# Decoder step: where a gate bias is added, where one weight split and one group of sums of squares stand

## The chip, the cores and the metric

The kernel runs on one core of one Trainium2 chip. The metric is the device time of one execution in microseconds (us), the median of several runs. TensorE (PE) does the matrix products, VectorE (DVE) and ScalarE (ACT) work element by element, GpSimd (POOL) and SyncE (SP) here mostly start transfers (DMA). Each engine runs its own list of instructions in order; semaphores make one wait for another. SBUF is the memory on the core, PSUM the memory into which TensorE writes.

## The reference, cut to what matters

Two layers over 256 prompt rows and 64 sample rows (8 sequences of 8), width 1024, all float32. The change touches the first half of a layer:

```python
z = h @ w_in[l]
u = gelu(z[..., :512]); v_raw = gelu(z[..., 512:1024]); p = z[..., 1024:]
# chunk_sgu: 4 heads x 128
v = head_layernorm(v_raw, g, b)
mixed = einsum('hts,bnshd->bnthd', w, vc) + bias      # bias = sgu_b[h, t]
ya = u * mixed
yb = pool_mix(...)                                    # windows 2/4/8/16, then a 128x128 product per group
mix = concatenate([rmsnorm(ya, branch_a_g), rmsnorm(yb, branch_b_g)]) @ w_out[l]
x = x + gt1 * mix
```

After it come a second norm and a SwiGLU, dense in layer 0, top-2-of-8 experts in layer 1.

## The kernel before

Activations lie transposed, channels on partitions and the 320 tokens along the free dimension. Every large weight matrix is read in units of 512x512 (1 MB) into a ring of six buffers `raw` by SP. ScalarE rounds a unit to `w_hi` (lines 709, 715), VectorE subtracts to get the remainder `w_lo` (lines 1052, 1057), and TensorE makes three products for each part: `w_hi` by the high part of the activation, `w_hi` by its low part, `w_lo` by the high part. `hi_to(s)` and `lo_to(s)` in the code mean: split all units up to number s that are not yet split, and where such a call stands in an engine's list decides what waits behind it. Units of `ada_w` are used as they are ("plain", line 1669, `ada`).

A layer's mixer half goes like this.

`project_in` multiplies six units, c = 0, 1, 2 for the pooling branch, v and u, two each, called j = 0 to 5. Ahead of unit j = 3 TensorE makes three of the four small products of the pooling branch (`mix_pool`, lines 1828 and 1829), which need VectorE's window differences (`pooled`, lines 1232 to 1246, semaphore `d_done`). `pooled` itself waits for ScalarE's copies of p (`p_out`, lines 810 to 815) and, half way, for GpSimd's window sums of the samples (`win_s`, line 621). On VectorE `lo_to(s + 4)`, the split of unit j = 3, stands ahead of `pooled`.

`mixer` makes the four heads of the gate (`mix_gate`). For a head: a product of a row of ones with the bias row for the 256 prompt columns (line 1814), the two products with the masked `gw` (1817), the bias product for the 64 sample columns (1819) and the sample product (1821). The bias row `g_bias` lies on one partition of `pst`. In layer 1 `mod_rows` (lines 1835, 1837) stands between heads 0 and 1; in layer 0 two `ada` units stand behind head 0 and two behind head 1. Behind the last head TensorE counts up `gate_mm`, on which VectorE forms `ya = u * gate` in one instruction (line 1278, reading PSUM), counts up `ya_done`, and goes on; ScalarE squares `ya` (line 861).

`project_out` multiplies four units of `w_out`, q = 0 to 3. The first two (q = 0, 1) take the rows of yb, which are ready; the last two take the rows of ya, which need its norm. Inside q = 0, after two of its four 128-row steps k (12 products each), TensorE waits for `ya_done` and the squares and makes their sums (`sum_squares`, line 1686), and in layer 0 the transposes of `ada_tr` (line 1679). Then ScalarE takes the root (741), VectorE the reciprocal (1252) and the scaled ya (1254), ScalarE and VectorE split it (795, 1264), and unit q = 2 can start.

GpSimd loads each layer's small parameters with `load_layer`; that of layer 1 starts when `gate_mm` says that layer 0's are used.

Of the kernel before, what the change touches and what calls it, by code (L numbers as in the profile page):

```python
# [30 lines left out]
P = 128  # L31
# [4 lines left out]
NSEQ = 8  # L36
# [13 lines left out]
BIAS_ROW = 96  # L50
# [96 lines left out]
def write_program(nc, ctx, d, o):  # L147
# [64 lines left out]
    g_bias = pst[BIAS_ROW:BIAS_ROW + 1].rearrange("p (h t) -> p h t", t=P)  # L212
# [345 lines left out]
    def _(gp):  # L558
# [8 lines left out]
        def load_layer(l):  # L567

            gp.dma_start(pw[:], d['pool_w'][l].rearrange("g c e -> c g e")).then_inc(layer_in, 16)
            gp.dma_start(g_bias, d['sgu_b'][l:l + 1]).then_inc(layer_in, 16)  # L570
            gp.dma_start(vng[:], d['v_norm_g'][l].partition_broadcast(P)).then_inc(layer_in, 16)
            gp.dma_start(vnb[:], d['v_norm_b'][l].partition_broadcast(P)).then_inc(layer_in, 16)
# [42 lines left out]
        for l in range(DEPTH):  # L615
# [18 lines left out]
            if l + 1 < DEPTH:  # L634
                gp.wait_ge(gate_mm, l + 1)
# [402 lines left out]
    def _(ve):  # L1038
# [146 lines left out]
        def project_in(l):  # L1185
# [10 lines left out]
            lo_to(s + 4)  # L1196
# [70 lines left out]
        def mixer(l):  # L1267
# [7 lines left out]
            branch_lo(H, 4 * l)  # L1275
            lo_to(S_OUT[l] + 3)
            ve.wait_ge(gate_mm, l + 1)
            v.tensor_tensor(uT[:], uT[:], ps[:, 0:H, 0:T], ALU.mult).then_inc(ya_done, 1)
# [363 lines left out]
    def _(pe):  # L1642
# [168 lines left out]
        def mix_gate(l, h):  # L1811
            hc = slice(h * P, (h + 1) * P)
            bias_one = ones[BIAS_ROW:BIAS_ROW + 1, :]
            t_.matmul(ps[:, h, 0:NP_TOK], bias_one, g_bias[:, h, :].unsqueeze(1).to_broadcast([1, 2, P]), start=True,
                      stop=False)
            for n in range(2):
                t_.matmul(ps[:, h, n * P:(n + 1) * P], v_norm[:, n, hc], gw[:, l, h, :], start=False, stop=(n == 1))
            tk = slice(NP_TOK, T)
            t_.matmul(ps[:, h, tk], bias_one, g_bias[:, h, 0:TS].unsqueeze(1).to_broadcast([1, NSEQ, TS]),
                      start=True, stop=False)  # L1820
            ins = t_.matmul(ps[:, h, tk], v_norm[NS_TOK:P, 2, hc], gs[NS_TOK:P, l, h, :], start=False, stop=True)
            if h == H - 1:
                ins.then_inc(gate_mm, 1)
# [32 lines left out]
        def project_out(l):  # L1856
# [7 lines left out]
            for q, (r, c) in enumerate(OUT_ORDER):  # L1864
# [13 lines left out]
                if q < N_OUT - 1:  # L1878
                    for k in range(KB):
                        if q == 0 and k == 2:  # L1880
                            pe.wait_ge(ya_done, l + 1)
                            sum_squares(12 * l + 2, 0, H, 0)
                            if l == 0:
                                ada_tr(SELF_B[0])
                        for m in range(4):
# [245 lines left out]
```

## Time and profile before

| | us |
|---|---|
| median of 3 runs | 1590.06 |
| lowest, highest | 1585.67, 1593.28 |
| profiled execution, its own time | 1592.71 |
| its span in the trace | 1591.0 |
| TensorE busy in the span | 1541.1 (97%) |
| VectorE, ScalarE busy | 1183.0, 946.6 |
| mean granted TensorE clock | 0.977 |

Layer 0's mixer half takes the first 160 us, the dense SwiGLU goes to about 470 us, layer 1's mixer half from there to about 595 us, and the experts take the rest. The trace gives start and duration of each instruction; matmuls overlap, so the distance between starts tells more than the duration. A float32 product (the gate, the sums of squares) shows as two matmul records, so "x4" there is two products. The granted clock is 1.00 at 2.4 GHz and 0.50 at 1.2 GHz. Times are counted from the start of the span.

### The profile page before, as it was taken

To read this page: it belongs to the slowest core of one execution; us is meant where nothing else is said; L and a number is where in the kernel's file an instruction comes from. 1 tells how busy PE (TensorE), PEld (TensorE's weight loads), DVE (VectorE), ACT (ScalarE), POOL (GpSimd) and SP (SyncE) were. 2 spreads that over 40 slices of the span, in tenths; PEclk is the share of its full clock that TensorE was granted. 3 is DMA by queue.
4 is the path that set the end of the run, shared out by engine and by line. 5 is a ranking of instruction groups with operands and counts; after the bars stand their busy time and mean duration, and the time that the engine had idled before them with its cause. 6 is when DMAs were issued, how large, how long until landed. Compare 5 with 4: busy or idle time off the path is not lost.

```text
span 1591.0 us, 21820 instructions
## 1 busy us (share of the span) xinstructions
PE 1541.1 (97%) x8061; PEld 1306.7 (82%) x8061; DVE 1183.0 (74%) x969; ACT 946.6 (59%) x721; POOL 70.7 (4%) x115
## 2 busy tenths in 40 slices
PE   6899999999998997999999999999999999999997
PEld 3669799999986796888888888888888888888785
DVE  3465544444465656888898898888888888889897
ACT  3343432333324534777777777777777777777774
POOL 4100000000000001000000000000000000001001
PEclk8999999999999996999999999999999999999999
DMA  9966764444439474999999999999999999999993
GB/s 344 377 241 251 293 244 136 154 158 133 157 110 382 149 255 133 377 375 370 390 381 370 394 379 366 400 372 377 392 371 371 403 371 373 395 374 367 398 377 134
DMA packets 234538, 493.00 MB, mean 310 GB/s; under 512 B 10219, under 2 KB 16235, under 8 KB 229370
## 3 DMA queue, kind: packets, MB, share of 16 engines
q1 hardware_dynamic: 226086, 472.82, 80.9%
q0 software_dynamic: 6112, 19.10, 3.2%
q10 hardware_dynamic: 2308, 0.64, 0.2%
q8 instruction: 21, 0.34, 0.1%
q14 instruction: 11, 0.09, 0.0%
HBM read 482.39 MB, written 10.36 MB: 310 GB/s over the span
## 4 chain that ended last, share of the span: by engine, by line
PE 90%; DMA 4%; DVE 3%; ACT 1%; issue 1%; SPq 0%; ACTq 0%; DVEq 0%
PE ps L1647 19%; PE ps L1649 19%; PE ps L1648 19%; PE ps L1915 4%; PE ps L1916 4%; PE ps L1917 4%; PE ps L1925 2%; PE ps L1926 2%; PE ps L1927 2%; DMA raw<-in_w_in 2%; PE ps L2068 2%; DMA raw<-in_ada_w 1%; PE ps L1874 1%; PE ps L1669 1%; PE ps L1875 1%; PE ps L1876 1%
## 5 line engine op out<-in xcount | busy, mean ns | idle before, releaser
L1057 DVE TENSOR_TENSOR w_lo<-raw,w_hi 128x2048 fp32r<-128x2048 f32 x366 | 835.2, 2291 | 178.9 <-ACT w_hi L715 177.7
L715 ACT ACTIVATE w_hi<-raw 128x2048 fp32r<-128x2048 f32 x366 | 701.9, 1918 | 263.7 <-PE ps L1649 162.1
L1647 PE MATMUL ps<-w_hi,split 128*128 128x512 f32 x1392 | 550.8, 396 | 2.1 <-DVE sp_ L1096 1.5
L1649 PE MATMUL ps<-w_hi,split 128*128 128x512 f32 x1392 | 544.0, 391 | 0.0
L1648 PE MATMUL ps<-w_lo,split 128*128 128x512 f32 x1392 | 543.6, 391 | 0.0
L1647 PEld LDWEIGHTS ps<-w_hi,split 128*128 128x128 f32 x1392 | 262.7, 189 | 58.8 <-DVE w_lo L1057 4.1
L1649 PEld LDWEIGHTS ps<-w_hi,split 128*128 128x128 f32 x1392 | 262.4, 189 | 55.6
L1648 PEld LDWEIGHTS ps<-w_lo,split 128*128 128x128 f32 x1392 | 262.9, 189 | 52.4
L1915 PE MATMUL ps<-split,w_hi 128*128 128x320 f32 x448 | 138.7, 310 | 1.9 <-DVE split L1162 1.9
L1917 PE MATMUL ps<-split,w_lo 128*128 128x320 f32 x448 | 138.4, 309 | 0.0
L1916 PE MATMUL ps<-split,w_hi 128*128 128x320 f32 x448 | 138.4, 309 | 0.0
L1052 DVE TENSOR_TENSOR w_lo<-raw,w_hi 128x2048 fp32r<-128x2048 f32 x32 | 73.3, 2293 | 69.9 <-ACT w_hi L709 69.9
L709 ACT ACTIVATE w_hi<-raw 128x2048 fp32r<-128x2048 f32 x32 | 60.9, 1908 | 51.2 <-PE ps L1917 17.1
L1915 PEld LDWEIGHTS ps<-split,w_hi 128*128 128x128 f32 x448 | 84.1, 188 | 3.6 <-issue 3.6
L1916 PEld LDWEIGHTS ps<-split,w_hi 128*128 128x128 f32 x448 | 84.1, 188 | 0.0
L1917 PEld LDWEIGHTS ps<-split,w_lo 128*128 128x128 f32 x448 | 84.1, 188 | 0.0
L983 ACT ACTIVATE split<-ps 128x512 fp32r<-128x512 f32 x56 | 33.5, 598 | 63.4 <-PE ps L2068 63.4
L1925 PE MATMUL ps<-split,w_hi 128*128 128x320 f32 x208 | 64.3, 309 | 0.0
L1926 PE MATMUL ps<-split,w_hi 128*128 128x320 f32 x208 | 64.3, 309 | 0.0
L1927 PE MATMUL ps<-split,w_lo 128*128 128x320 f32 x208 | 64.3, 309 | 0.0
L1669 PE MATMUL ps<-raw,cT 128*32 128x512 f32 x384 | 48.3, 623 | 8.8 <-DMA raw<-in_ada_w 8.8
L1800 PE MATMUL ps<-split,w_hi 128*128 128x320 f32 x128 | 41.7, 326 | 3.4 <-DVE split L1162 1.8
(342 smaller groups left out, 1297.8 us busy)
## 6 DMA issues: line engine op xcount, KB each, us to landing
raw<-in_moe_w SPq DMA_DIRECT2D x336, 1024.0 KB, 7.3
raw<-in_ffn_w SPq DMA_DIRECT2D x42, 1024.0 KB, 5.0
raw<-in_ada_w SPq DMA_DIRECT2D x40, 1024.0 KB, 7.2
raw<-in_w_in SPq DMA_DIRECT2D x12, 1024.0 KB, 11.0
raw<-in_ada_w SPq DMA_DIRECT2D x16, 512.0 KB, 10.7
raw<-in_w_out SPq DMA_DIRECT2D x8, 1024.0 KB, 8.9
item_rows<-plain POOLq DMA_DIRECT2D x12, 512.0 KB, 7.8
plain<-in_x_prompt SPq DMA_DIRECT2D x2, 512.0 KB, 3.8
```

The costliest lines, as they stand in the source:

```text
L715: a.activation(w_hi[:, (s0 + j) % SPL], raw[:, (u0 + j) % RAW], ACT.Copy).then_inc(hi_ready, 1)
L1052: v.tensor_tensor(w_lo[:, s % SPL], raw[:, u % RAW], w_hi[:, s % SPL].bitcast(F32), ALU.subtract).then_inc(lo_ready, 1)
L1057: v.tensor_tensor(w_lo[:, (s0 + j) % SPL], raw[:, (u0 + j) % RAW], w_hi[:, (s0 + j) % SPL].bitcast(F32), ALU.subtract).then_inc(lo_ready, 1)
L1647: t_.matmul(out, a_hi, b_hi, start=first_, stop=False)
L1648: t_.matmul(out, a_hi, b_lo, start=False, stop=False)
L1649: return t_.matmul(out, a_lo, b_hi, start=False, stop=last_)
L1915: t_.matmul(out, wh[:, k, mc], h_hi[:, kk, 0:T], start=(kk == 0), stop=False)
L1916: t_.matmul(out, wh[:, k, mc], h_lo[:, kk, 0:T], start=False, stop=False)
L1917: ins = t_.matmul(out, wl[:, k, mc], h_hi[:, kk, 0:T], start=False, stop=(kk == KD - 1))
L1925: t_.matmul(out, wh[:, k, mc], gh[:, k, :], start=(k == 0), stop=False)
L1926: t_.matmul(out, wh[:, k, mc], gl[:, k, :], start=False, stop=False)
L1927: ins = t_.matmul(out, wl[:, k, mc], gh[:, k, :], start=False, stop=(k == KB - 1))
```

## The change

The bias goes to a buffer of its own that holds it on all 128 partitions, loaded by a transfer that repeats the row. The two bias products of each head are gone. VectorE adds the bias to the gate in two instructions (256 prompt columns and 64 sample columns of each of four heads), waits for them, and then multiplies with u. This block stands ahead of the split of output unit q = 2 (`lo_to(S_OUT[l] + 3)`) and behind that of q = 1; before, the product stood behind both. GpSimd's `load_layer(1)` waits for `ya_done`, since VectorE now reads the bias. On TensorE the sums of squares stand after three steps k of unit q = 0, with `ada_tr` ahead of them. And in `project_in` the call `lo_to(s + 4)` ahead of `pooled` is made in layer 0 alone; in layer 1 the split of unit j = 3 falls behind `pooled`.

```diff
-    g_bias = pst[BIAS_ROW:BIAS_ROW + 1].rearrange("p (h t) -> p h t", t=P)
+    g_bias = sb("g_bias", [P, H, P])
...
-            gp.dma_start(g_bias, d['sgu_b'][l:l + 1]).then_inc(layer_in, 16)
+            gp.dma_start(g_bias[:].rearrange("p h t -> p (h t)"),
+                         d['sgu_b'][l].rearrange("h t -> (h t)").partition_broadcast(P)).then_inc(layer_in, 16)
...
-                gp.wait_ge(gate_mm, l + 1)
+                gp.wait_ge(ya_done, l + 1)
...
-            lo_to(s + 4)
+            if l == 0:
+                lo_to(s + 4)
             pooled(l)
...
             branch_lo(H, 4 * l)
+            lo_to(S_OUT[l] + 2)
+            ve.wait_ge(gate_mm, l + 1)
+            gated = hf[:, 0:H, :]
+            v.tensor_tensor(gated[:, :, 0:NP_TOK].rearrange("p h (n t) -> p h n t", t=P),
+                            ps[:, 0:H, 0:NP_TOK].rearrange("p h (n t) -> p h n t", t=P),
+                            g_bias[:].unsqueeze(2).to_broadcast([P, H, 2, P]), ALU.add)
+            step(v.tensor_tensor(gated[:, :, NP_TOK:T].rearrange("p h (n t) -> p h n t", t=TS),
+                                 ps[:, 0:H, NP_TOK:T].rearrange("p h (n t) -> p h n t", t=TS),
+                                 g_bias[:, :, 0:TS].unsqueeze(2).to_broadcast([P, H, NSEQ, TS]), ALU.add))
+            v.tensor_tensor(uT[:], uT[:], gated, ALU.mult).then_inc(ya_done, 1)
             lo_to(S_OUT[l] + 3)
-            ve.wait_ge(gate_mm, l + 1)
-            v.tensor_tensor(uT[:], uT[:], ps[:, 0:H, 0:T], ALU.mult).then_inc(ya_done, 1)
...
-            t_.matmul(ps[:, h, 0:NP_TOK], bias_one, g_bias[:, h, :].unsqueeze(1).to_broadcast([1, 2, P]), start=True,
-                      stop=False)
             for n in range(2):
-                t_.matmul(ps[:, h, n * P:(n + 1) * P], v_norm[:, n, hc], gw[:, l, h, :], start=False, stop=(n == 1))
-            tk = slice(NP_TOK, T)
-            t_.matmul(ps[:, h, tk], bias_one, g_bias[:, h, 0:TS].unsqueeze(1).to_broadcast([1, NSEQ, TS]),
-                      start=True, stop=False)
-            ins = t_.matmul(ps[:, h, tk], v_norm[NS_TOK:P, 2, hc], gs[NS_TOK:P, l, h, :], start=False, stop=True)
+                t_.matmul(ps[:, h, n * P:(n + 1) * P], v_norm[:, n, hc], gw[:, l, h, :], start=True, stop=True)
+            ins = t_.matmul(ps[:, h, NP_TOK:T], v_norm[NS_TOK:P, 2, hc], gs[NS_TOK:P, l, h, :], start=True, stop=True)
...
-                        if q == 0 and k == 2:
+                        if q == 0 and k == 3:
                             pe.wait_ge(ya_done, l + 1)
-                            sum_squares(12 * l + 2, 0, H, 0)
                             if l == 0:
                                 ada_tr(SELF_B[0])
+                            sum_squares(12 * l + 2, 0, H, 0)
```

On VectorE in layer 1, around the pooling differences. Before, with the splits of j = 2 and j = 3 as "x2":

```order
L1052 TENSOR_TENSOR w_lo<-raw,w_hi 128x2048 x2
L1232 TENSOR_TENSOR plain<-pp 128x4x270
L1232 TENSOR_TENSOR plain<-plain 128x3x268
L1232 TENSOR_TENSOR plain<-plain 128x2x264
L1232 TENSOR_TENSOR plain<-plain 128x256
L1238 SCALAR_TENSOR_TENSOR plain<-plain,pp 128x240
```

After, where `pooled` ends and the splits of j = 3 and j = 4 follow as "x2" (its start has one split ahead of it):

```order
L1239 SCALAR_TENSOR_TENSOR plain<-plain,pp 128x240
L1241 SCALAR_TENSOR_TENSOR plain<-plain,sp_ 128x8x8
L1243 TENSOR_TENSOR first<-plain,rcnt 128x16
L1247 TENSOR_TENSOR plain<-first,pp 128x16 x4
L1052 TENSOR_TENSOR w_lo<-raw,w_hi 128x2048 x2
L1204 BN_STATS v_stat<-plain 128x6 x12
```

One split has moved from ahead of `pooled` to behind it.

On TensorE in layer 1, from the last transposes of `project_in` to gate head 1. `ps<-pst,ones` is a bias product, `ps<-mix,plain` a gate product. Before:

```order
L1814 MATMUL ps<-pst,ones 128x256
L1817 MATMUL ps<-mix,plain 128x128 x2
L1819 MATMUL ps<-pst,ones 128x64
L1821 MATMUL ps<-mix,plain 128x64
L1835 MATMUL ps<-ident,gain 72x128
L1835 MATMUL ps<-ident,mod 72x128 x2
L1837 MATMUL ps<-rw,mod 9x8 x8
L1814 MATMUL ps<-pst,ones 128x256
```

After:

```order
L1823 MATMUL ps<-mix,plain 128x128 x2
L1824 MATMUL ps<-mix,plain 128x64
L1838 MATMUL ps<-ident,gain 72x128
L1838 MATMUL ps<-ident,mod 72x128 x2
L1840 MATMUL ps<-rw,mod 9x8 x8
L1823 MATMUL ps<-mix,plain 128x128 x2
```

Both bias products are gone from each head.

On TensorE in layer 0, inside output unit q = 0 (`w_hi` and `w_lo` with `split` are its products). Before, where the unit's first product is row 331:

```order
353 L1875 MATMUL ps<-split,w_hi 128x320
354 L1876 MATMUL ps<-split,w_lo 128x320
355 L1686 MATMUL ps<-hf,ones 128x320 x4
356 L1679 MATMUL ps<-ident,modrow 128x128 x4
357 L1874 MATMUL ps<-split,w_hi 128x320
```

After, where its first product is row 323:

```order
357 L1878 MATMUL ps<-split,w_hi 128x320
358 L1879 MATMUL ps<-split,w_lo 128x320
359 L1688 MATMUL ps<-ident,modrow 128x128 x4
360 L1695 MATMUL ps<-hf,ones 128x320 x4
361 L1877 MATMUL ps<-split,w_hi 128x320
```

The sums have moved from behind 24 products to behind 36, and the transposes stand ahead of them.

## Rows read from the trace of the kernel before

**Rows 1.** Page, part 1: engine, busy us, share of the span, instructions.

```profile
PE 1541.1 (97%) x8061; PEld 1306.7 (82%) x8061; DVE 1183.0 (74%) x969; ACT 946.6 (59%) x721; POOL 70.7 (4%) x115
```

**Rows 2.** Groups by line, 600 to 1591 us: busy, mean ns, idle before by releaser.

```profile
L715 ACT ACTIVATE w_hi<-raw 128x2048 fp32r<-128x2048 f32 x334 | 640.7, 1918 | 166.0 <-PE ps L1649 162.1 <-DMA raw<-in_moe_w 3.7 <-issue 0.3
L1647 PE MATMUL ps<-w_hi,split 128*128 128x512 f32 x1344 | 530.6, 395 | 0.6 <-DVE w_lo L1057 0.6
```

**Rows 3.** Timelines of ACT, POOL, DVE and PE around layer 1's `pooled`: start, us.

```profile
499.15 0.28 ACT L815 ACTIVATE hf<-ps 128x60 f32<-128x60 f32 x1
500.95 2.12 POOL L621 TENSOR_TENSOR plain<-plain 128x480 f32<-128x480 f32 x3
503.86 2.29 DVE L1052 TENSOR_TENSOR w_lo<-raw,w_hi 128x2048 fp32r<-128x2048 f32 x1 [5.93 <-ACT w_hi L709]
506.07 1.28 DVE L1232 TENSOR_TENSOR plain<-pp 128x1080 f32<-128x1080 f32 x1
511.90 0.43 DVE L1246 TENSOR_TENSOR plain<-first,pp 128x16 f32<-128x16 f32 x4
512.38 0.70 PE L1828 MATMUL ps<-plain,mix 128*128 128x256 f32 x2 [2.76 <-DVE plain L1246]
```

**Rows 4.** Stretches: length, busy of PE, PEld, DVE, ACT, POOL, granted clock, DMA, GB/s.

```profile
20.00:40.00 20.00, 11.79 (x67) 6.62 (x68) 8.78 (x14) 5.95 (x8) 4.23 (x7) 0.74 1.06 378
...
124.00:132.00 8.00, 8.00 (x33) 7.56 (x33) 3.69 (x2) 3.08 (x4) 2.43 (x4) 0.57 1.04 412
...
513.00:518.00 5.00, 5.00 (x20) 4.21 (x19) 0.26 (x1) 3.65 (x5) 0.00 (x0) 0.66 1.01 406
547.00:551.00 4.00, 3.02 (x31) 2.13 (x30) 3.79 (x6) 2.19 (x3) 0.00 (x0) 1.00 0.00 0
551.00:565.00 14.00, 14.00 (x46) 10.67 (x45) 6.62 (x4) 6.06 (x7) 0.00 (x0) 0.51 0.69 156
```

**Rows 5.** Timeline of PE in layer 0, gate heads 2 and 3.

```profile
120.00 1.06 PE L1669 MATMUL ps<-raw,cT 128*32 128x512 f32 x8 [1.36 <-DMA raw<-in_ada_w]
120.99 0.69 PE L1814 MATMUL ps<-pst,ones 1*128 1x256 f32 x2
121.62 0.71 PE L1817 MATMUL ps<-mix,plain 128*128 128x128 f32 x4
122.26 0.43 PE L1819 MATMUL ps<-pst,ones 1*128 1x64 f32 x2
122.62 0.43 PE L1821 MATMUL ps<-mix,plain 64*128 64x64 f32 x2
```

**Rows 6.** Timeline of PE in layer 1: gate, output unit q = 0, sums.

```profile
548.08 0.67 PE L1814 MATMUL ps<-pst,ones 1*128 1x256 f32 x2 [0.98 <-ACT plain L848]
...
561.43 0.63 PE L1874 MATMUL ps<-split,w_hi 128*128 128x320 f32 x1
...
566.57 2.31 PE L1686 MATMUL ps<-hf,ones 128*128 128x320 f32 x8
...
569.16 0.30 PE L1874 MATMUL ps<-split,w_hi 128*128 128x320 f32 x1
...
577.08 0.31 PE L1874 MATMUL ps<-split,w_hi 128*128 128x320 f32 x1
```

**Rows 7.** Timelines of DVE and ACT in layer 1, from the gate's end.

```profile
553.45 4.50 DVE L1052 TENSOR_TENSOR w_lo<-raw,w_hi 128x2048 fp32r<-128x2048 f32 x2 [1.81 <-ACT w_hi L709]
561.53 1.49 DVE L1278 TENSOR_TENSOR plain<-plain,ps 128x1280 f32<-128x1280 f32 x1 [3.59 <-PE ps L1821]
569.48 2.15 DVE L1252 RECIPROCAL rstd<-rstd 128x320 f32<-128x320 f32 x1 [6.46 <-ACT rstd L741]
573.53 1.72 DVE L1264 TENSOR_TENSOR split<-hf,split 128x640 fp32r<-128x640 f32 x2
563.05 1.36 ACT L861 ACTIVATE hf<-plain 128x640 f32<-128x640 f32 x2 [7.84 <-DVE plain L1278]
```

**Rows 8.** Chain of work that ended last, in order of time: start, us, what.

```profile
49.31 13.53 DMA raw<-in_w_in
```

More of the change, by code:

```diff
@@ L49 @@
 WIN = (2, 4, 8, 16)
-BIAS_ROW = 96
 PADP = 16
@@ L1812, in mix_gate @@
             hc = slice(h * P, (h + 1) * P)
-            bias_one = ones[BIAS_ROW:BIAS_ROW + 1, :]
-            t_.matmul(ps[:, h, 0:NP_TOK], bias_one, g_bias[:, h, :].unsqueeze(1).to_broadcast([1, 2, P]), start=True,
-                      stop=False)
             for n in range(2):
-                t_.matmul(ps[:, h, n * P:(n + 1) * P], v_norm[:, n, hc], gw[:, l, h, :], start=False, stop=(n == 1))
-            tk = slice(NP_TOK, T)
-            t_.matmul(ps[:, h, tk], bias_one, g_bias[:, h, 0:TS].unsqueeze(1).to_broadcast([1, NSEQ, TS]),
-                      start=True, stop=False)
-            ins = t_.matmul(ps[:, h, tk], v_norm[NS_TOK:P, 2, hc], gs[NS_TOK:P, l, h, :], start=False, stop=True)
+                t_.matmul(ps[:, h, n * P:(n + 1) * P], v_norm[:, n, hc], gw[:, l, h, :], start=True, stop=True)
+            ins = t_.matmul(ps[:, h, NP_TOK:T], v_norm[NS_TOK:P, 2, hc], gs[NS_TOK:P, l, h, :], start=True, stop=True)
             if h == H - 1:
```

## The prediction, made before the changed kernel was run

> **What bounds the kernel now.** I read the engines' busy times first, then who waits for whom, then the timeline of each stretch that the diff touches. TensorE is busy 97% of the span [rows 1]. In the experts it idles 0.6 us over 1344 products of a line, and ScalarE waits for it (162 us), not for weights (3.7 us) [rows 2]. So whatever TensorE gains ahead of the experts reaches the end, unless something takes it back on the way. Two of its losses matter here. It idles 2.76 us in layer 1 for VectorE's pooling differences [rows 3]. And its clock falls from 2.4 to 1.2 GHz (granted share 0.5) in three stretches beside the change [rows 4]: 124 to 132 us at a mean of 0.57, that is 2 x 0.43 x 8 = 6.9 us at the low level; 513 to 518 at 0.66, 3.4 us; 551 to 565 at 0.51, 13.7 us. Time at the low level costs at most half of itself.
>
> **The pooling differences in layer 1.** Before, the split of unit j = 3 waits 5.93 us for ScalarE and runs 503.86 to 506.15, and `pooled` runs 506.07 to 512.33 [rows 3]. What `pooled` itself needs is there earlier: ScalarE's copies at 499.43, GpSimd's sums at 503.07 [rows 3]. Without the split ahead of it, it ends by 503.1 + 6.3 = 509.4 even if all of it waited for the sums, and near 506 if its first half runs before them. TensorE comes free 2.76 us before 512.38, at 509.6, so this idle time goes: **2.8 us**. What is late next is the split of j = 3: it ends 2.3 us behind `pooled`, at 508.3 (at 511.7 at worst). TensorE needs it behind three pooling products, 512.38 to 515.11 at part low clock, near 2.1 us at full, so at 511.7. No wait. SP's next load hangs on TensorE's `ada` units there, at 508.8, not on this split. The low clock from 513 on followed that idle time with TensorE otherwise at work; with it gone I count its 3.4 us x 0.5 = **1.6 us** as saved too. Together 4.4; between 2.8 and 4.5.
>
> **The bias products.** A head's first costs 121.62 - 120.99 = 0.63 us and its second 122.62 - 122.26 = 0.36 us at full clock [rows 5], together 0.99. Layer 1 has four heads with nothing between them but `mod_rows`: 3.96 us. In layer 0 heads 0 and 1 lie ahead of an `ada` unit whose load lands at 120.0, where TensorE already waits 1.36 us [rows 5]; the transfers are saturated there, and their issue lies ahead of the gate. Their 1.98 us only lengthen that wait. Heads 2 and 3 lie behind it: **2.0 us**.
>
> **The clock in layer 1.** From 547 to 551 TensorE idles 0.98 us and is else busy with small gate products, and it is at the low level from 551 to 565: through three heads and half of unit q = 0, until the large products have run for 3 us [rows 4, 6]. After the change the thin stretch shrinks from 548.1-561.4 to 548.1-553.0 at full clock (4.0 for four bare heads, 0.9 for `mod_rows`). The nearest row of such a length is layer 0's, with 6.9 us at the low level; I take that. Saved: (13.7 - 6.9) x 0.5 = 3.4. The bounds are 0 (it stays low as long) and 6.8 (it does not fall). With 3.96 that makes **7.4 us** for layer 1's gate. In layer 0 I leave the clock as it was, though its thin stretch changes too: TensorE waits 3.3 us in all for loads in place of 1.4, and then has less thin work; bounds 3.4 either way.
>
> The Trainium skill (TensorE: Matmul & The Clock Gate, section "Why this matters for your kernels") says that the clock drops after an idle gap between bursts of matmuls. The idle gap of 2.76 us bears that out; the fall at 551, after 0.98 us of idle and with products in every other slot, does not. By that rule alone, layer 1's gate would stay at full clock.
>
> **VectorE's added steps.** The old product takes 1.49 us for 1280 columns read from PSUM, and 640 columns take 0.86 (two in 1.72) [rows 7]. By these the adds of 1024 and 256 columns take near 1.2 and 0.4, 1.6 together with a wait, and the product 1.5: **3.1 us** from `gate_mm` to `ya_done`, off TensorE's path if covered. In layer 1: the second of the splits at 553.45 now stands behind, the first moves up with `mod_rows` by 1.0, to end near 554.8; `ya_done` near 557.9, squares (1.36, [rows 7]) near 559.3. TensorE starts q = 0 at 553.0 and makes 36 products. At full clock 54 products take 577.08 - 569.16 = 7.92 us [rows 6], 0.147 each, so 36 take 5.3: arrival 558.3, plus 3.4 for low clock = 561.7. Cover 2.4 us; at full clock a wait of 1.0. In layer 0 the split of q = 2 no longer stands ahead, adds and squares take 4.5, and 36 products take 5.3 or more: covered. That split comes up to 3 us later, for a unit that TensorE reaches over 10 us later. Waiting here also are GpSimd's loads for layer 1, needed 350 us on, and ScalarE's squares.
>
> **The sums one step later.** They cost TensorE the same. What gets shorter is the cover of the root, reciprocal, scaling and split behind them: 575.25 - 568.9 = 6.3 us [rows 7]. TensorE has 12 + 48 products left ahead of q = 2, 8.8 us. Before it had 72, 10.6. Cost 0, cover 2.5. If VectorE were 2.5 us late there it would be the path.
>
> **The larger load.** 256 KB in place of 2 KB, in layer 0 at 32 us, when the transfers run at 378 GB/s and a share of 1.06 [rows 4]. The chain goes through such a load later, 49.31 to 62.84 [rows 8]. 0.254 MB by 378 GB/s is **0.7 us**, lost; bounds 0 and 1.4 (if the repeated row goes at half the rate). Layer 1's copy is in nobody's way.
>
> **Sum.** 4.4 + 2.0 + 7.4 - 0.7 = 13.1 us off. The profiled execution took 1592.7, 2.65 above the median of 1590.06; by its own time it would be 1579.6. Against the median: **1577.0 us**.
>
> **Rivals.** (a) The clock does not fall in layer 1's gate, since the small products keep it up. The saving is 6.8 in place of 3.4 and the wait for the squares costs 1.0: 1574.6; if layer 0's does not fall either, 3.4 less, 1571.2. For it: the stretch is a third as long. Against it: the fall at 551 came 3 us into such work. The Trainium skill (TensorE: Matmul & The Clock Gate, "Why this matters for your kernels"), which names idle gaps alone, would give (a) for layer 1. (b) The clock gives nothing back: low in layer 1 up to the same products (3.4 more), and in layer 0 also during the loads' wait (3.4 more): 1577.0 + 6.8 = 1583.8. For it: layer 0 now idles 3.3 us where 2.76 went with a fall [rows 3, 4]. Against it: the large products come 8 us sooner in layer 1. (c) The idle time before the pooling products only changes its releaser, to the split of j = 3 or the row sums: 4.4 back, 1581.4. Against it are the times above. (d) The gain is lost in the experts, where the transfers are nearly full: 1590. Against it stands the 0.6 us [rows 2]. (e) Slower: the add with a repeated operand runs at the rate of VectorE's slowest row, the reciprocal, 2.15 us for 320 columns [rows 7]. The adds then take 8.6 in place of 1.6. In layer 1 the squares end 7.0 later, 4.6 behind TensorE's arrival at 561.7. In layer 0 the gate's end to the squares takes 11.5 against 8.7 of products with the low clock: 2.8. Two waits of that size each bring back up to 3.4 of low clock: 4.6 + 2.8 + 6.8 = 14.2, more than the 13.1 saved: 1591.2. It decides from about 8 us for the adds on. Against it: the same kind of instruction with PSUM takes 1.49 for 1280.
>
> **How the numbers follow.** The forecast 0.52, (a) 0.13, (b) 0.18, (c) 0.06, (d) 0.06, (e) 0.05. About 8 us, 0.5%, is what a measurement of this kernel can tell from no change, so faster means under 1582.1: the forecast, (a), (c) and half of (b) hold 0.80, from which I take 0.03 for scatter of the median: 0.77. Within 0.5%: the rest of (b), (d), most of (e): 0.20. Slower 0.03. The range goes from (a)'s lower end, 1571, to 1585, past (b); (d), (e) and scatter, under 0.2, are left out.
>
> **What would show it.** In the profile of after: no idle time ahead of layer 1's first pooling product and a clock of 1.00 behind it, or (c). Between the starts of two neighbouring heads 1.0 us. Adds of 1.2 and 0.4 us, or (e). No idle time ahead of either layer's sums of squares and of unit q = 2; a wait there means that VectorE's chain is the path. The low clock near layer 1's gate 3 to 7 us long; 13 is (b), none is (a). TensorE's wait in layer 0's second pair of `ada` units near 3.3 us. The first large products some 0.7 us later up to 80 us. What would prove me wrong altogether: the experts lasting longer than before by what was gained.

## The result and the profile after

| | us |
|---|---|
| before, same chip, 4 runs | 1590.60 (1585.67 to 1593.28) |
| after, 4 runs | 1573.58 (1571.84 to 1577.49) |
| ratio | 0.9914, 95% interval 0.9895 to 0.9934 |
| profiled execution of after, its span | 1577.49, 1575.7 |

The change takes 17.0 us off the median, where 13.1 were forecast. The profiled pair lies 15.2 us apart, which is what the traces have to explain.

First the page of after, part 1, which answers to [rows 1], and the groups by line from 600 us on, which answer to [rows 2].

```profile
PE 1528.3 (97%) x8029; PEld 1297.2 (82%) x8029; DVE 1188.1 (75%) x973; ACT 946.5 (60%) x721; POOL 73.4 (5%) x115
...
L715 ACT ACTIVATE w_hi<-raw 128x2048 fp32r<-128x2048 f32 x334 | 640.7, 1918 | 165.4 <-PE ps L1658 163.0 <-DMA raw<-in_moe_w 2.0 <-issue 0.3
```

TensorE has 32 records and 12.8 us less to do, VectorE 4 instructions and 5.1 us more. In the experts ScalarE still waits 163 us for TensorE and 2.0 us for weights. So TensorE is the bound there as before.

**Where the time went.** I cut the span at eight starts that both kernels have on TensorE. These rows are of before (start, duration, engine, line, what): the `ada` unit ahead of layer 0's pooling products, the one ahead of its gate, the sums of x behind unit q = 3, the `ada` units ahead of and behind layer 1's unit j = 3, and the transposes of x behind layer 1's mixer. Between the first two stands the start of layer 0's pooling products. Layer 1's gate begins at 548.08 [rows 6].

```profile
69.20 1.92 PE L1669 MATMUL ps<-raw,cT 128*32 128x512 f32 x16
73.91 1.22 PE L1828 MATMUL ps<-plain,mix 128*128 128x256 f32 x2 [2.78 <-DVE plain L1246]
109.89 1.92 PE L1669 MATMUL ps<-raw,cT 128*32 128x512 f32 x16
158.84 0.43 PE L1686 MATMUL ps<-hf,ones 128*128 128x320 f32 x1
507.70 1.50 PE L1669 MATMUL ps<-raw,cT 128*32 128x512 f32 x12
524.36 1.06 PE L1669 MATMUL ps<-raw,cT 128*32 128x512 f32 x8
593.36 0.49 PE L1987 MATMUL ps<-ident,x 128*128 128x128 f32 x3
```

The same places on TensorE in after, with its gates between them. What stands in brackets is idle time before the row and what ended it.

```profile
71.64 1.92 PE L1678 MATMUL ps<-raw,cT 128*32 128x512 f32 x16
74.75 0.70 PE L1831 MATMUL ps<-plain,mix 128*128 128x256 f32 x2 [1.18 <-DVE plain L1247]
107.78 1.92 PE L1678 MATMUL ps<-raw,cT 128*32 128x512 f32 x16
115.77 1.51 PE L1678 MATMUL ps<-raw,cT 128*32 128x512 f32 x8 [2.20 <-DMA raw<-in_ada_w]
118.25 1.93 PE L1678 MATMUL ps<-raw,cT 128*32 128x512 f32 x8 [0.97 <-DMA raw<-in_ada_w]
155.78 0.43 PE L1695 MATMUL ps<-hf,ones 128*128 128x320 f32 x1
504.64 1.92 PE L1678 MATMUL ps<-raw,cT 128*32 128x512 f32 x16
506.49 0.48 PE L1831 MATMUL ps<-plain,mix 128*128 128x256 f32 x1
516.86 0.64 PE L1678 MATMUL ps<-raw,cT 128*32 128x512 f32 x4
540.58 0.68 PE L1823 MATMUL ps<-mix,plain 128*128 128x128 f32 x4 [0.98 <-ACT plain L848]
578.87 0.38 PE L1990 MATMUL ps<-ident,x 128*128 128x128 f32 x2
```

And in a second trace of after, the same program without an edit, profiled on another chip (1570.36 us by its own time, span 1568.5):

```profile
70.78 1.92 PE L1678 MATMUL ps<-raw,cT 128*32 128x512 f32 x16
108.49 1.92 PE L1678 MATMUL ps<-raw,cT 128*32 128x512 f32 x16
114.97 1.06 PE L1678 MATMUL ps<-raw,cT 128*32 128x512 f32 x8 [0.69 <-DMA raw<-in_ada_w]
117.45 1.07 PE L1678 MATMUL ps<-raw,cT 128*32 128x512 f32 x8 [1.42 <-DMA raw<-in_ada_w]
151.31 0.43 PE L1695 MATMUL ps<-hf,ones 128*128 128x320 f32 x1
501.31 1.92 PE L1678 MATMUL ps<-raw,cT 128*32 128x512 f32 x16
513.53 1.05 PE L1678 MATMUL ps<-raw,cT 128*32 128x512 f32 x6
537.25 0.68 PE L1823 MATMUL ps<-mix,plain 128*128 128x128 f32 x4 [0.98 <-ACT plain L848]
547.84 2.39 PE L1695 MATMUL ps<-hf,ones 128*128 128x320 f32 x8
572.94 0.49 PE L1990 MATMUL ps<-ident,x 128*128 128x128 f32 x3
```

The differences of neighbouring starts, in us:

| stretch | before | after | after, second trace |
|---|---|---|---|
| A: start to layer 0's unit j = 3 | 69.20 | 71.64 | 70.78 |
| B: to layer 0's gate | 40.69 | 36.14 | 37.71 |
| C: layer 0's gate and output product | 48.95 | 48.00 | 42.82 |
| D: to layer 1's unit j = 3 | 348.86 | 348.86 | 350.00 |
| E: pooling products and unit j = 3 | 16.66 | 12.22 | 12.22 |
| F: to layer 1's gate | 23.72 | 23.72 | 23.72 |
| G: layer 1's gate and output product | 45.28 | 38.29 | 35.69 |
| H: to the end | 997.64 | 996.83 | 995.56 |

In the first trace 4.44 us went in E, 6.99 in G, 0.95 in C, 2.11 in A and B together and 0.81 in H. That is the 15.3 us between the spans. F stays the same to 0.01 us, and so does D where the clock is the same.

The last two columns are one program, and they differ by 7.2 us. Most of that is granted clock. These rows are stretches of after, then of its second trace: length, busy time of PE, PEld, DVE, ACT and POOL, granted clock, DMA share, GB/s.

```profile
60.00:66.00 6.00, 4.35 (x12) 3.52 (x13) 1.98 (x4) 1.92 (x1) 4.10 (x5) 0.72 1.03 425
110.00:130.00 20.00, 16.83 (x90) 11.24 (x89) 8.88 (x7) 7.44 (x7) 2.42 (x4) 0.74 1.01 393
540.00:555.00 15.00, 14.42 (x84) 12.69 (x85) 11.65 (x10) 8.47 (x10) 0.00 (x0) 0.77 0.54 131
```

```profile
110.00:130.00 20.00, 17.89 (x119) 12.90 (x116) 10.39 (x10) 8.69 (x9) 2.43 (x4) 1.00 1.01 389
...
470.00:480.00 10.00, 8.12 (x51) 7.24 (x42) 7.09 (x14) 8.95 (x13) 0.00 (x0) 0.83 1.02 411
```

A mean of 0.74 over 20 us is 2 x 0.26 x 20 = 10.4 us at 1.2 GHz. The first trace has 3.4, 10.4 and 6.9 us at this level in the three stretches. The second has none there and 3.4 us at 470. What the low level costs can be read where TensorE makes the same work with and without it:

| same work | with low clock | without | cost |
|---|---|---|---|
| G, both traces of after | 38.29, 6.9 low | 35.69 | 2.60 |
| C from the last `ada` load (118.25, 117.45) on, both traces of after | 37.53, 8.2 low | 33.86 | 3.67 |
| layer 0's pooling products to the gate's `ada` unit, before and first after | 35.98, 6.8 low | 33.03 | 2.95 |

That is 0.38 to 0.45 of its length, a little under the half that the prediction's terms took; the 3.4 us at 470 cost 1.14 us in D. The other 1.51 of the 5.18 us by which the two traces differ in C is not clock: TensorE waits 2.20 us for the load at 115.77 in the first and 0.69 us at 114.97 in the second.

### The profile page after: what moved, and what is told of

It reads as the page before. It is cut to its first block, busy times and chain, and to the rows that moved or that the text cites. A ratio compares the mean times of both kernels' runs of the same rounds, so it can differ in the third digit from the quotient of the medians.

```text
span 1575.7 us, 21759 instructions
## 1 busy us (share of the span) xinstructions
PE 1528.3 (97%) x8029; PEld 1297.2 (82%) x8029; DVE 1188.1 (75%) x973; ACT 946.5 (60%) x721; POOL 73.4 (5%) x115
## 4 chain that ended last, share of the span: by engine, by line
PE 92%; DMA 3%; DVE 3%; ACT 1%; issue 0%; SPq 0%; DVEq 0%; ACTq 0%
PE ps L1656 20%; PE ps L1658 20%; PE ps L1657 20%; PE ps L1918 4%; PE ps L1919 4%; PE ps L1920 4%; PE ps L1928 2%; PE ps L1929 2%; PE ps L1930 2%; DMA raw<-in_ada_w 2%; PE ps L2071 2%; PE ps L1678 1%; PE ps L1877 1%; PE ps L1878 1%; PE ps L1879 1%; PE ps L1695 1%
## 6 DMA issues: line engine op xcount, KB each, us to landing
raw<-in_ada_w SPq DMA_DIRECT2D x16, 512.0 KB, 10.6
```

## The experiments

All kernels of one batch ran on one chip, with before timed beside them. The first four below are the first batch, the next four the second, the others the third; the kernel after was timed again in the third alone. The first batch's before has a median of 1588.36 us, the second's 1587.01, the third's 1586.2. 

### Each part of the change alone

**The load alone**, on before:

```diff
+    g_all = sb("g_all", [P, H, P])
+    g_bias = g_all[BIAS_ROW:BIAS_ROW + 1]
...
-            gp.dma_start(g_bias, d['sgu_b'][l:l + 1]).then_inc(layer_in, 16)
+            gp.dma_start(g_all[:].rearrange("p h t -> p (h t)"),
+                         d['sgu_b'][l].rearrange("h t -> (h t)").partition_broadcast(P)).then_inc(layer_in, 16)
```

> Only the load is changed against the kernel before: the bias row is repeated on all 128 partitions (256 KB in place of 2 KB), and the gate's products still add it from one partition. Theory A (the forecast): the opening is bound by transfers, so 0.7 us slower, bounds 0 and 1.4; the first product of layer 1's units 0.7 us later. Rival B (the opening gained 2.1 us in the changed kernel because the larger load shifts the transfers): 2 us faster. Rival C (those 2.1 us are chance, from when TensorE's clock falls near 62 and 74 us): within 2 us either way, and the place of the low clock in the opening differs from that of the kernel before.

Measured: 1590.46 us (10 runs), ratio 1.0003 (0.9982 to 1.0025). The time can't tell 0.7 us from none, but the place does. TensorE comes to the `ada` unit ahead of unit j = 3 at 69.96 us in place of 69.20:

```profile
69.96 1.92 PE L1671 MATMUL ps<-raw,cT 128*32 128x512 f32 x16
```

In the twelve traces with the large load this start lies between 69.33 and 71.64 us, with 70.1 in the middle. In the two without it, before and the next kernel, it lies at 69.20 and 69.06. So the load costs about 1.0 us, by twelve traces against two.

**The split alone**, on before:

```diff
-            lo_to(s + 4)
+            if l == 0:
+                lo_to(s + 4)
             pooled(l)
```

> Only the split of unit j = 3 is moved behind the pooling differences in layer 1. Theory A: 4.4 us faster (2.8 of idle time, 1.6 of low clock behind it); no idle time ahead of the first pooling product. Rival: the split is then late and TensorE waits for it behind the pooling products: 2.8 us of idle time come back there, and the gain is under 2 us.

Measured: 1584.8 us (10 runs), ratio 0.9975 (0.9958 to 0.9992), 3.6 us off. TensorE in layer 1:

```profile
509.58 0.48 PE L1829 MATMUL ps<-plain,mix 128*128 128x256 f32 x1
...
519.94 0.64 PE L1670 MATMUL ps<-raw,cT 128*32 128x512 f32 x4
```

The first pooling product starts without idle time. The `ada` unit behind j = 3 comes at 519.94 in place of 524.36, with the one ahead at 507.72 (before: 507.70). So 4.44 us go in this stretch, the same as in after. One moved call is the whole of it.

**The bias on VectorE alone**, with its block and the load, on before. The split of j = 3 and the sums stay where they were:

```diff
-            lo_to(S_OUT[l] + 3)
+            lo_to(S_OUT[l] + 2)
             ve.wait_ge(gate_mm, l + 1)
-            v.tensor_tensor(uT[:], uT[:], ps[:, 0:H, 0:T], ALU.mult).then_inc(ya_done, 1)
+            gated = hf[:, 0:H, :]
...
+            v.tensor_tensor(uT[:], uT[:], gated, ALU.mult).then_inc(ya_done, 1)
+            lo_to(S_OUT[l] + 3)
```

> Only the bias goes to VectorE (with the larger load and its block ahead of output unit 2's split); the split of j = 3 and the sums of squares stand as before. Theory A: 2.0 + 7.4 - 0.7 = 8.7 us faster, less what TensorE waits for the squares in layer 1, which it reaches 1.8 us sooner than in the changed kernel: after the changed kernel's 1.6 us of cover that is 0 to 0.5 us. Rival B: the sums' place matters more, and TensorE waits 2 us and more in both layers, 5 us faster.

Measured: 1579.93 us (6 runs), ratio 0.9949 (0.9927 to 0.9971), 8.4 us off. TensorE in layer 1:

```profile
508.32 0.70 PE L1830 MATMUL ps<-plain,mix 128*128 128x256 f32 x2 [2.65 <-DVE plain L1246]
...
552.98 2.39 PE L1694 MATMUL ps<-hf,ones 128*128 128x320 f32 x8 [1.88 <-ACT hf L861]
```

The idle time ahead of the pooling products is back, but no low clock follows it here. Ahead of the sums stands a new wait of 1.88 us: behind 24 products they come too early for the adds. The clock in layer 1's gate is 1.00.

**Sums of squares at their old place**, on after:

```diff
-                        if q == 0 and k == 3:
+                        if q == 0 and k == 2:
                             pe.wait_ge(ya_done, l + 1)
+                            sum_squares(12 * l + 2, 0, H, 0)
                             if l == 0:
                                 ada_tr(SELF_B[0])
-                            sum_squares(12 * l + 2, 0, H, 0)
```

> The changed kernel with the sums of squares back behind two steps of output unit 0, ahead of ada_tr. Theory A: as fast as the changed kernel within 1 us (17 us faster than before), with an idle time ahead of the sums of under 1 us in layer 1 and none in layer 0. Rival B: the excess over my forecast (17.0 for 13.1) comes from this step: 13 us faster than before, with idle time of 2 us ahead of the sums in each layer.

Measured: 1572.53 us (4 runs), ratio 0.9897 (0.9866 to 0.9928), so not slower than after by its time. TensorE in layer 0 and layer 1, and ScalarE's squares of layer 1:

```profile
123.27 2.12 PE L1695 MATMUL ps<-hf,ones 128*128 128x320 f32 x7 [0.33 <-ACT hf L861]
...
547.13 3.90 PE L1695 MATMUL ps<-hf,ones 128*128 128x320 f32 x8 [1.88 <-ACT hf L861]
...
546.25 1.36 ACT L861 ACTIVATE hf<-plain 128x640 f32<-128x640 f32 x2 [3.54 <-DVE plain L1286]
```

The trace decides where the time can't. The waits of 1.88 and 0.33 us are there, and low clock follows the first: the sums take 3.90 us in place of 2.39. From the first gate head (536.54) to the transposes of x (575.67) it takes 39.13 us, where the second trace of after takes 35.69. So in layer 1 the later place was worth 3.4 us between these two traces, once the adds are there. In the time of whole executions this is hidden by the scatter of the clock elsewhere. Here the clock is 1.00 from 105 to 135 us, where the first trace of after has 0.83. Of the 3.4 us only the 1.88 us of wait come every time: in the kernel with the bias alone the same wait brought no fall, and its sums took 2.39 us.

### VectorE's adds: how much is covered

**The block behind the split of q = 2**, on after (the old order of VectorE):

```diff
-            lo_to(S_OUT[l] + 2)
+            lo_to(S_OUT[l] + 3)
             ve.wait_ge(gate_mm, l + 1)
...
             v.tensor_tensor(uT[:], uT[:], gated, ALU.mult).then_inc(ya_done, 1)
-            lo_to(S_OUT[l] + 3)
```

> The changed kernel with VectorE's block (both adds and the product) back behind the split of output unit 2. Theory A (the order is worth only what TensorE's cover does not hide): in layer 1 ya_done comes 2.3 us later against a cover of 1.8 us in the changed kernel's trace, in layer 0 up to 3 us later (that split waits for its load) against 2.5: 0 to 1.5 us slower than the changed kernel, with idle time of under 1 us ahead of the sums. Rival B (the order carries the excess over the forecast): 4 us slower.

Measured: 1575.68 us (4 runs), ratio 0.9929 (0.9912 to 0.9946). TensorE ahead of layer 0's transposes and sums, and ScalarE's squares in layer 1:

```profile
129.39 0.66 PE L1687 MATMUL ps<-ident,modrow 128*128 128x128 f32 x4 [1.27 <-DVE plain L1286]
...
552.03 1.37 ACT L861 ACTIVATE hf<-plain 128x640 f32<-128x640 f32 x2 [5.75 <-DVE plain L1286]
```

In layer 0 TensorE waits 1.27 us for VectorE's product, at a clock of 1.00; neither trace of after has a wait there. So in layer 0 the block's place ahead of the split saves 1.3 us here. In layer 1 no idle time stands ahead of the sums, but TensorE was late itself: the clock from 541 to 551 us is 0.55. The first square ends near 552.7. At full clock TensorE would have been at the sums 10.6 us behind the first head (540.12), at 550.7, and would have waited about 2 us. That wait I worked out; this run didn't show it. The time, 11.3 us below before, can't tell this kernel from after.

**The adds made four times**, on after, 4.9 us more for VectorE in each layer:

```diff
+            for _ in range(4):
+                v.tensor_tensor(gated[:, :, 0:NP_TOK]...
+                step(v.tensor_tensor(gated[:, :, NP_TOK:T]...
```

> The changed kernel with the two adds made four times over (same result each time), so that VectorE's block lasts 4.9 us longer in each layer. Theory A: TensorE waits ahead of the sums for what exceeds its cover, 4.9 - 1.8 = 3.1 us in layer 1 and 4.9 - 2.5 = 2.4 us in layer 0, and each wait may bring up to 1.7 us of low clock: 5.5 to 9 us slower than the changed kernel. Rival B (VectorE's block is on the path already): 9.8 us slower and more. Rival C (it is hidden altogether): under 2 us.

Measured: 1581.61 us (10 runs), ratio 0.9964 (0.9946 to 0.9983). TensorE in layer 0 and layer 1:

```profile
129.54 1.08 PE L1689 MATMUL ps<-ident,modrow 128*128 128x128 f32 x4 [2.47 <-DVE plain L1287]
...
556.92 0.87 PE L1696 MATMUL ps<-hf,ones 128*128 128x320 f32 x1 [4.89 <-ACT hf L861]
```

In layer 1 all of the 4.9 us added is waited for, at a clock of 1.00: the adds have no cover left there. In layer 0 it is 2.47 of 4.9, so 2.4 are covered. What follows runs at the low clock for a while. From the first head (541.56) to the transposes of x (585.01) it takes 43.45 us against 35.69, 7.8 more for 4.9 of idle time. This is rival (e) at work, and by its time the kernel is only 5.4 us faster than before, where after is 12.2 and 17.0. It did not come with the change because the two adds take 1.6 us together, far from the 8 from which it decides.

### The clock in layer 1's gate

**One gate head in place of four**, layer 1, on after. Three of the four heads' gates are left out there:

```diff
             for h in range(H):
-                mix_gate(l, h)
+                if l == 0 or h == H - 1:
+                    mix_gate(l, h)
```

> The changed kernel with three of layer 1's four gate heads left out (part of the computation is missing; mod_rows and head 3 stay, and so does the idle time of 1 us ahead of the gate). Theory A (the small products pull TensorE's clock down): besides their 3.0 us the low clock of 6.8 us beside layer 1's gate goes, or shrinks to 3.4: 4.7 to 6.4 us faster than the changed kernel, less up to 2 us of wait for the squares. Rival B (the idle time ahead of the gate pulls it down, as the skill's rule on idle gaps has it): the clock still falls there, 3 us faster at most.

Measured: 1569.97 us (4 runs), ratio 0.9892 (0.9876 to 0.9909). In layer 1 the heads leave, and waits of TensorE for VectorE of 1.09 us (ahead of 543.09) and 1.62 us (ahead of 546.70) take their place. The mean clock from 543 to 553 us is 0.83, so it falls for 3.4 us even so. This run was meant to tell whether thin products or idle time bring the fall. It has less of the one and more of the other, so it doesn't tell. Rival B of the expectation also asks more of the Trainium skill (TensorE: Matmul & The Clock Gate, section "Why this matters for your kernels") than the prediction found there: by the prediction's reading an idle time of 0.98 us brings no fall.

All traces together tell more. The mean granted clock in layer 1 from about the first gate head to about the sums:

| kernels | clock in that stretch |
|---|---|
| with the bias products: before, load alone, split alone | 0.62, 0.58, 0.64 |
| without them, four heads: bias alone, sums at the old place, adds four times, three variants below and one again, second trace of after | 1.00 in all eight |
| without them: after, block behind the split | 0.76, 0.66 |

All have the same 0.98 us of idle time ahead of the gate. With the bias products the clock falls every time, for 13.7 to 16.8 us. Without them it falls in two of ten. The kernels with the products also have a longer gate, by 4.0 us, so the table does not say whether the shape of these products or the length of the thin stretch matters.

### Layer 0: two further edits, and after once more

**Gate heads 1 to 3 ahead of the last two `ada` units**, on after, so that the wait for their load is filled:

```diff
-                if l == 0 and h < 2:
-                    ada(SELF_B[0], 2 * h + 4, 2 * h + 6)
+                if l == 0 and h == 0:
+                    ada(SELF_B[0], 4, 6)
+            if l == 0:
+                ada(SELF_B[0], 6, 8)
```

> The changed kernel with layer 0's gate heads 1 to 3 ahead of the last two ada units, so that TensorE makes them while it waits for these loads. Theory A: in the changed kernel's trace it waits 2.2 and 1.0 us for the loads, and heads 2 and 3 take 3.5 us behind them at the low clock, so 2 to 3.5 us come off, less up to 0.9 us of wait for ScalarE's copy of the ada row: 1.5 to 3 us faster than the changed kernel. Rival B (the transfers set the end of this stretch whatever TensorE does, and the clock takes the rest): under 1 us.

Measured: 1568.09 us (4 runs), ratio 0.9886 (0.9868 to 0.9903). TensorE in layer 0:

```profile
118.46 0.38 PE L1879 MATMUL ps<-split,w_hi 128*128 128x320 f32 x1 [0.76 <-issue]
```

The `ada` units (from 115.72) run without a wait for their load; 0.76 us of idle time stand behind them. I ran it again in the third batch, beside after:

> The kernel after with gate heads 1 to 3 of layer 0 ahead of the last two ada units, once more, on the same chip as after, for the comparison of the two. If the order of the heads is worth its time (the wait for the load filled with 2 us of gate products, and less low clock behind it), it is 3 to 5.5 us below after: ratio to after 0.9965 to 0.998. If that was a clock that happened to stay up, it is within 1.5 us of after.

Measured: 1570.85 us (5 runs), ratio 0.9904 (0.9889 to 0.9920).

```profile
121.45 1.07 PE L1678 MATMUL ps<-raw,cT 128*32 128x512 f32 x8 [1.41 <-DMA raw<-in_ada_w]
```

This time the load came later, and a wait of 1.41 us stayed. Stretch C takes 41.3 us in the first of the two runs and 43.1 in the second, against 42.8 in the second trace of after. The order itself gains in both. From the last load on, TensorE needs 32.67 us to the end of C in the second run (121.45 to 154.12) and 33.86 in the second trace of after, both at full clock: 1.2 us less, the two heads' 2.0 less the new idle time of 0.76. In the first run it is 1.5 us over the whole of C. What hid it in the second run is when the load landed: 10.44 us behind the start of C, against 8.96 in the second trace of after; in the nine traces with the large load and the old order this lies anywhere between 8.7 and 10.6. The rest of the first run's lead was the clock, 1.00 from 105 to 135 us. By the medians of the third batch the kernel lies 3.1 us below after (ratio 0.9980, with 0.9967 to 1.0010 by drawing anew from the times of each), so the time doesn't confirm the gain.

**The split of j = 3 between the halves of `pooled`**, layer 0, on after:

```diff
-            if l == 0:
-                lo_to(s + 4)
             pooled(l)
...
                 src = dst
+            if l == 0:
+                lo_to(S_IN[l] + 4)
             ve.wait_ge(win_s, l + 1)
```

> The kernel after, with one line moved in layer 0: VectorE's split of unit j = 3 goes from ahead of the pooling differences to between their two halves (behind the first half, which needs ScalarE's copies alone, ahead of the wait for GpSimd's sums). In the profile of after VectorE idles 4.02 us ahead of that split (65.61 us) while the copies are there from 59.86. Theory A: in layer 0 too TensorE only waits for the order on VectorE, and the load that TensorE waits for later (116 to 118 us) is issued when an ada unit frees its buffer, so it comes as much earlier: the idle time of 1.2 to 2.8 us ahead of layer 0's pooling products goes and all that follows comes 1.2 to 2.8 us sooner; ratio to after 0.998 to 0.999. Rival B: the transfers are the limit up to 120 us; the idle time ahead of the pooling products goes and the wait for the ada load grows by as much; same time as after (ratio 1.000). Rival C: the first half beside GpSimd's sums takes longer (4.2 us in layer 1 where 2.2 is the usual) and pushes the split: no more than 1 us gained.

Measured: 1568.73 us (6 runs), ratio 0.9896 (0.9876 to 0.9916). VectorE, then TensorE, in layer 0:

```profile
62.11 4.35 DVE L1231 TENSOR_TENSOR plain<-plain 128x804 f32<-128x804 f32 x3
66.50 2.96 DVE L1052 TENSOR_TENSOR w_lo<-raw,w_hi 128x2048 fp32r<-128x2048 f32 x1
...
73.17 0.48 PE L1831 MATMUL ps<-plain,mix 128*128 128x256 f32 x1 [1.92 <-DVE plain L1247]
```

The idle time is 1.92 us, 0.8 less than the 2.73 to 2.79 of the nine traces with the large load in which this order is the old one and TensorE is not late itself: rival C of the expectation. The first half now runs beside GpSimd and takes 4.35 us where it takes 2.2 alone, the split 2.96 where it takes 2.3, and then VectorE waits 0.95 us for GpSimd's own sums. The 5.2 us by which the median lies below after's in the same batch can't come from 0.8 us of work.

**Both**, on after:

> The kernel after with both further changes in layer 0: gate heads 1 to 3 stand ahead of the last two ada units, and the split of unit j = 3 stands between the halves of the pooling differences. Theory A: the two gains add: 5 us of the first (as in the run with the heads alone, 1568.1) and 1.2 to 2.8 of the second, so 1565 to 1567, ratio to before 0.987. Rival B (transfers are the limit up to 120 us): with the heads moved nothing is left over from the second, 1568. Rival D: the gain of the heads was a clock that happened to stay up; then this lies at 1570 to 1573, like after.

Measured: 1568.0 us (6 runs, 1564.5 to 1573.79), ratio to before 0.9897 (0.9876 to 0.9919). Its trace takes 1564.7 us, 3.8 less than the second trace of after: 0.8 from the pooling products, 1.4 in stretch C, 0.65 in A and the rest from a low clock at 470 us that it doesn't have. It is the fastest of its batch. It beats before for sure. Against after in that batch the ratio of medians is 0.9962, with 0.9944 to 1.0006 by drawing anew from the six times of each. So some 2 us of gain are seen in the trace, and the time can't confirm them.

**After again:**

> The kernel after, unchanged, on the same chip as its variants, and a second trace of it. My reading of the first trace is that the idle time ahead of layer 1's pooling products is gone for good and that the places where the clock falls in layer 0 differ from execution to execution. Then here the pooling products of layer 1 follow without idle time again and no low clock stands behind them, while the stretches of low clock up to 130 us lie elsewhere or have another length than 31 to 38, 62 to 65 and 116 to 127 us. If the clock is a fixed answer to the program, all stretches repeat. Time 1572 to 1577, ratio to before 0.989 to 0.993.

Measured: 1573.97 us (6 runs, 1568.73 to 1576.13), ratio 0.9924 (0.9906 to 0.9943). The mean granted clock of these six, all on one chip, goes from 0.982 to 0.987. The trace is the one shown above. Layer 1's pooling products follow without idle time again, and none of the first trace's three low stretches behind 60 us is there.

## Why the prediction was right

**What bounds the kernel.** Right. Stretches D and F are the same to 0.01 us in the two first traces, and H keeps all that was gained: nothing was given back in the experts, rival (d).

**The pooling differences, 4.4 us.** Right, with 4.44 us in after, in its second trace and with the split alone. VectorE in layer 1:

```profile
496.42 1.28 DVE L1233 TENSOR_TENSOR plain<-pp 128x1080 f32<-128x1080 f32 x1 [1.45 <-ACT hf L815]
497.74 4.24 DVE L1233 TENSOR_TENSOR plain<-plain 128x804 f32<-128x804 f32 x3
...
504.91 2.28 DVE L1052 TENSOR_TENSOR w_lo<-raw,w_hi 128x2048 fp32r<-128x2048 f32 x1
```

`pooled` starts as soon as the copies are there and ends at 505.0, 1.5 us ahead of TensorE, between the 506 and the 509.4 of the prediction (3.06 less here, since all starts that much sooner: 502.9 and 506.3). It was later than 502.9 for a reason that I had not seen: the additions behind the first take 4.24 us beside GpSimd's sums, where they take 2.2 in layer 0. Rival (c) did not come: the split of j = 3 ends at 507.2 and nobody waits for it. But the 4.4 is made of 2.8 that always comes and 1.6 that depends on the clock. In the kernel with the bias alone the same idle time of 2.65 us brings no fall, and there the split would have been worth 2.7.

**The gate of layer 1, 7.4 us.** 6.99 in the first trace and 9.6 in the second. The part without the clock, four heads at 0.99, stands: in the second trace two neighbouring heads start at 539.16 and 540.17 us. The part of the clock I took from one row as one number, and it differs from trace to trace. Of ten traces without the bias products eight have no fall ahead of the sums. The other two have 6.9 and 10.2 us at the low level, where I had taken 6.9. That the first trace agrees with this term to 0.4 us is luck. So (a) was the likelier mechanism, and I gave it 0.13. It did not show in the predicted time as much as it might have, since 3.4 us are only a fifth of a per cent.

The rule of the Trainium skill that I weighed there (TensorE: Matmul & The Clock Gate, section "Why this matters for your kernels") says that idle gaps drop the clock, and by it this gate would have stayed at full clock. For the kernel without bias products the traces agree in eight of ten. For the one with them they don't: three of three fall, with the same 0.98 us of idle time ahead. So the bias products had a share in it, by their one row of weights or by the 4.0 us that they add to the gate. No run here tells which.

**The wait for the squares.** Rival (a) came with a wait of 1.0 us for the squares at full clock. It did not come. These rows are VectorE and ScalarE in the second trace of after, where it takes 10.59 us from the first gate head to the sums:

```profile
543.85 1.22 DVE L1280 TENSOR_TENSOR hf<-ps,g_bias 128x1024 f32<-128x1024 f32 x1
544.98 0.41 DVE L1283 TENSOR_TENSOR hf<-ps,g_bias 128x256 f32<-128x256 f32 x1
...
546.96 1.36 ACT L861 ACTIVATE hf<-plain 128x640 f32<-128x640 f32 x2 [3.54 <-DVE plain L1286]
```

Adds of 1.22 and 0.41 and a product of 1.49: 3.07 us, as forecast (1.2, 0.4, 1.5). The squares end at 548.32, 11.07 us behind the first head, against 11.2 forecast. TensorE arrives after 10.59, and starts at once, since its first sums need the first of the two squares alone (with the sums at the old place they start at 547.13, while the squares run from 546.25 to 547.61). The working put all of them behind both. Rival (e) fell with the 1.22.

**The sums one step later, 0.** Right for what the sums cost TensorE: 2.31 us before, 2.31 and 2.39 after in layer 1. But with the adds the step also saves the wait of 1.88 us in layer 1, and more where the clock falls behind it. The cover of 2.5 us behind them held: no idle time stands ahead of unit q = 2 in either layer.

**Layer 0's heads, 2.0 us.** Right. Heads 2 and 3 stand behind the last `ada` load. From there to the end of C it takes 38.84 us before (120.00 [rows 5] to 158.84), 37.53 in the first trace of after and 33.86 in the second. The second is 4.98 us shorter and has no low clock, where before has 6.9 us [rows 4]. At the 0.43 us for each us that the low level cost at the pooling products (2.95 for 6.8), 3.0 of it are clock and 2.0 the heads. The first is 1.31 us shorter with 1.3 us more of low clock, which gives 1.9. The rest of C is when that load lands: 10.11 us behind the start of C before, 10.47 and 8.96 after. In the first trace the time of heads 0 and 1 only made the wait longer, as forecast: 2.20 and 0.97 us against 1.36 [rows 5], 3.2 in all (3.3 forecast). In the second it is 0.69 and 1.42, so there more was gained than forecast.

**The load, -0.7 us.** About -1.0, inside the bounds.

**What no term had.** A and B gave 2.1 us in the first trace. TensorE starts layer 0's pooling products 0.84 us later than before (74.75 against 73.91), and needs 33.03 us from there to the gate's `ada` unit in place of 35.98. That is the low clock: before has 6.8 us of it behind the idle time of 2.78 us there, after has none. In the first trace of after this idle time is 1.18 us only, since TensorE comes late itself (71.64). In the second it is 2.75, as before, and no fall follows either. I don't take this for an effect of the change: eleven traces have an idle time of about 2.75 us in that place, and the clock falls behind it in five, two of them without the large load (both fall) and nine with it (three fall). That is too few to tie it to the load. In the third batch after lies 12.2 us below before, where the first measurement has 17.0, and the forecast of 13.1 lies between them. The split alone and the bias alone gave 3.6 and 8.4. So I read the 3.9 us above the forecast as scatter, most of it of the clock. That is argued: only one execution of the first measurement has a trace. What was wrong in the working is that I gave the clock a term where it needed a spread.

## What to carry to other kernels

Look on the side engine for a call that stands ahead of something TensorE waits for and has its own inputs later: moving it behind cost nothing in this kernel, and one moved call gave 2.8 us, 4.4 with the clock. Where a step is moved off the busiest engine onto a covered one, move its consumer back by the time it takes, in the same edit; without that, 1.9 us of idle time came in its place. And take two traces of one program before a difference of a few us between two kernels gets a cause.

## What the runs showed of the hardware

**The clock differs between executions of one program.** The two traces of after have 20.7 and 3.4 us of low clock between 60 and 580 us, and 7.2 us between their spans; they ran on different chips, but six executions on one chip also go from 0.982 to 0.987 in mean clock and from 1576.13 to 1568.73 us in time. An idle time of about 2.75 us in layer 0 is followed by 3.6 to 6.8 us at 1.2 GHz in five of eleven traces and by none in the others. These are the same 12 us of the kernel with the heads moved, in its second run and its first:

```profile
73.00:85.00 12.00, 10.04 (x34) 8.39 (x35) 4.17 (x14) 4.66 (x5) 0.00 (x0) 0.72 0.62 253
```

```profile
73.00:85.00 12.00, 10.04 (x47) 8.49 (x48) 4.16 (x14) 4.67 (x5) 0.00 (x0) 1.00 0.63 252
```

Both have TensorE busy for 10.04 us, and the one at 0.72 has 34 matmul records in it where the other has 47.

**VectorE and GpSimd slow each other.** The three additions at 804 columns and less take 2.2 us alone, 4.24 and 4.35 beside GpSimd's additions. The split of 2.3 us takes 2.96 there. GpSimd's sums in layer 1 take 1.35 and 2.12 us before, where VectorE is idle, and 2.45 and 3.17 in after, beside VectorE's additions. The Trainium skill (SBUF — State Buffer, section "Who interferes with whom") says that a VectorE instruction with two inputs in SBUF contends with a GpSimd instruction that reads SBUF; the traces agree, by these numbers.
